# The sparse-attention mixer of a three-block fp32 network: negated scores in PSUM, maxima by pair, and a respaced step list

## What is computed

```python
q, kc, vc, ks, vs, kw, vw, gt, cf = split(h @ w_in)        # 8 q heads, 2 kv groups, head_dim 64
gates = sigmoid(gt).reshape(b, t, 8, 3)
q, ks, kw = rope(rms_norm(q)), rope(rms_norm(ks)), rope(rms_norm(kw))
# compressed branch: 15 blocks of 32 tokens (stride 16), flattened to 2048
kc = rms_norm(gelu(blocks(rope(kc)) @ cmp_w1[0]) @ cmp_w2[0])
vc = gelu(blocks(vc) @ cmp_w1[1]) @ cmp_w2[1]
o_cmp = masked_softmax(q @ kc.T / 8, block_end <= pos) @ vc
# with 256 tokens all 4 selection blocks are chosen and the window covers all: both plain causal attention
o_slc = softmax(q @ ks.T / 8 + causal) @ vs
o_win = softmax(q @ kw.T / 8 + causal) @ vw
o = gates[0] * o_cmp + gates[1] * o_slc + gates[2] * o_win
# convolution branch
z = a * sigmoid(b)                                          # a, b = split(cf), 512 channels each
z = silu(layer_norm(causal_dwconv(z, conf_dw /* 31 taps */) + conf_dw_b))
x = x + concat([o, z]) @ w_out
```

## Time and profile before

| | |
|---|---|
| median of three timed runs | 1105.21 us (1097.91, 1105.21, 1107.57) |
| profiled execution, device time | 1110.08 us |
| its span | 1108.3 us |
| mean granted TensorE clock | 0.950 |
| TensorE busy | 1030.8 us, 93% |
| VectorE, ScalarE, GpSimd busy | 613.7, 492.9, 194.7 us |
| chain that ended last | TensorE 83%, VectorE 6%, ScalarE 5%, GpSimd 3% |

### The profile page before, as it was taken

The page is one execution under the profiler, slowest core; times in us unless marked ns, Lnnn a source line. Parts: engine busy times, 40 slices in busy tenths (PEclk is TensorE's granted clock), DMA queues, the critical chain, the costliest instruction groups (busy, mean ns, idle before and its releaser), DMA issues.

```text
span 1108.3 us, 16443 instructions
## 1 busy us (share of the span) xinstructions
PE 1030.8 (93%) x6750; PEld 916.6 (83%) x6750; DVE 613.7 (55%) x830; ACT 492.9 (44%) x688; POOL 194.7 (18%) x185
## 2 busy tenths in 40 slices
PE   5998999999898888879999998999999999699998
PEld 5987999999788677669999997777777778699996
DVE  4764554454587694345454455455655555755664
ACT  5335444344444443444344344455554545345452
POOL 0006910000122021100000000333442503400000
PEclk9998999999898795699999999999999999899999
DMA  8653565656554320034655665454435543544260
GB/s 277 197 174 115 190 190 184 194 185 192 162 183 150 114 75 2 1 113 142 195 186 175 194 212 172 147 171 134 143 123 171 159 146 107 160 154 136 93 227 39
DMA packets 120273, 168.61 MB, mean 152 GB/s; under 512 B 6356, under 2 KB 89364, under 8 KB 120212
## 3 DMA queue, kind: packets, MB, share of 16 engines
q1 hardware_dynamic: 119776, 167.58, 47.0%
q10 hardware_dynamic: 436, 0.19, 0.1%
HBM read 165.29 MB, written 2.46 MB: 151 GB/s over the span
## 4 chain that ended last, share of the span: by engine, by line
PE 83%; DVE 6%; ACT 5%; POOL 3%; issue 2%; DMA 1%; SPq 0%; DVEq 0%; ACTq 0%; POOLq 0%
PE ps L397 25%; PE ps L399 24%; PE ps L398 24%; PE ps L635 3%; PE ps L609 2%; PE ps L623 2%; ACT scratch_sb L673 1%; DVE scratch_sb L1097 1%; DVE wlo_sb L386 1%; POOL sinv_sb L462 1%; PE ps L785 1%; ACT whi_sb L380 1%; POOL scratch_sb L1986 1%; DMA scratch_sb<-conf_dw 1%; POOL b_inv_sb L1980 1%
## 5 line engine op out<-in xcount | busy, mean ns | idle before, releaser
L386 DVE TENSOR_TENSOR wlo_sb<-raw_sb,whi_sb 128x2048 fp32r<-128x2048 f32 x150 | 345.2, 2301 | 220.7 <-ACT whi_sb L380 220.6
L380 ACT ACTIVATE whi_sb<-raw_sb 128x2048 fp32r<-128x2048 f32 x150 | 287.0, 1914 | 201.2 <-PE ps L399 198.1
L397 PE MATMUL ps<-hhi_sb,whi_sb 128*128 128x256 f32 x1088 | 310.0, 285 | 11.0 <-DVE qkl_sb L1867 7.2
L398 PE MATMUL ps<-hlo_sb,whi_sb 128*128 128x256 f32 x1088 | 308.1, 283 | 0.0
L399 PE MATMUL ps<-hhi_sb,wlo_sb 128*128 128x256 f32 x1088 | 307.5, 283 | 0.0
L397 PEld LDWEIGHTS ps<-hhi_sb,whi_sb 128*128 128x128 f32 x1088 | 209.2, 192 | 14.8 <-DVE wlo_sb L386 7.4
L398 PEld LDWEIGHTS ps<-hlo_sb,whi_sb 128*128 128x128 f32 x1088 | 209.2, 192 | 0.8
L399 PEld LDWEIGHTS ps<-hhi_sb,wlo_sb 128*128 128x128 f32 x1088 | 209.0, 192 | 0.0
L397 PE MATMUL ps<-whi_sb,hhi_sb 128*128 128x512 f32 (+1 forms) x336 | 135.0, 402 | 1.5 <-DVE hlo_sb L479 1.4
L398 PE MATMUL ps<-wlo_sb,hhi_sb 128*128 128x512 f32 (+1 forms) x336 | 131.1, 390 | 0.0
L399 PE MATMUL ps<-whi_sb,hlo_sb 128*128 128x512 f32 (+1 forms) x336 | 131.1, 390 | 0.0
(11 more groups left out here) (270 smaller groups left out, 1237.1 us busy)
## 6 DMA issues: line engine op xcount, KB each, us to landing
raw_sb<-w_in SPq DMA_DIRECT2D x45, 1024.0 KB, 5.3
raw_sb<-ffn_gate SPq DMA_DIRECT2D x22, 1024.0 KB, 5.3
raw_sb<-ffn_up SPq DMA_DIRECT2D x22, 1024.0 KB, 5.2
raw_sb<-ffn_down SPq DMA_DIRECT2D x22, 1024.0 KB, 4.9
raw_sb<-w_in_odd SPq DMA_DIRECT2D x9, 1024.0 KB, 5.2
raw_sb<-w_in_even SPq DMA_DIRECT2D x8, 1024.0 KB, 7.1
raw_sb<-w_branch SPq DMA_DIRECT2D x6, 1024.0 KB, 5.1
scratch_sb<-bias_rows_dram SPq DMA_DIRECT2D x40, 128.0 KB, 2.7
```

The lines of the kernel that those rows point to most:

```text
L380: nc.scalar.activation(whi[:, n0 % SPLIT, :], raw[:, n0 % RAW, :], ACT.Copy).then_inc(hi_ready, 1)
L386: nc.vector.tensor_tensor(wlo[:, n0 % SPLIT, :], raw[:, n0 % RAW, :], whi[:, n0 % SPLIT, :].bitcast(F32), ALU.subtract).then_inc(lo_ready, 1)
L397: nc.tensor.matmul(dst, l_hi, r_hi, start=first, stop=False)
L398: nc.tensor.matmul(dst, l_hi, r_lo, start=False, stop=False)
```

## The change

Nothing outside the odd mixer changes. In it:

1. **Scores.** q's scale is negative, so that PSUM holds negated scores. The mask is added by TensorE: one product of the identity with the negated 128 x 128 mask, both as float32r copies that ScalarE writes into `hhi[:, 2]` (`ident_r`, `mask_r`). Only the last 128 columns need it. VectorE takes the minimum of both heads in one reduction from PSUM, ScalarE's exponentials read PSUM. Pairs alternate between banks 0, 1 and 2, 3, and the transposes go into the pair's own first bank. So scores of pair p wait for the copy of pair p-2, no longer for VectorE's operation on p-1.
2. **Order.** The compressing tiles are whole at steps -2, 0, 6 and 8 (before: -2, -1, 2, 3); the wait for q and k moves behind the first. The tiles are split at other steps (`SPLIT_STEP`). The fourth group's convolution goes one step in two, from 1 to 27. VectorE does two taps a step. `rope_k` and its sums go ahead of a split, both token copies and flat blocks one tile earlier.
3. **Tail.** Layer norm, second branch sum and output rows leave the step list (now -2 to 32) and stand behind it. Output rows begin with the attention half. The last value products are weighted out of PSUM by VectorE, GpSimd keeps one of that sum's products. ScalarE's table loads for the root and for Silu are triggered ahead of their waits by operations on one column.

```diff
+        ident_r, mask_r = hhi[:, 2, 0:P], hhi[:, 2, P:T]
...
+        def pair_s1(pe, p):
+            if p >= 2:
+                pe.wait_ge(pT_copied, p - 1)
+            two, b = jobs1[2 * p:2 * p + 2], 2 * (p % 2)
+            w = len(two[0][5]) * P
+            for e, (qh, ql, kh, kl, bias, v, g, col) in enumerate(two):
+                nc.tensor.matmul(ps[:, b + e, 0:w], qh, kh, start=True, stop=False)
+                nc.tensor.matmul(ps[:, b + e, w - P:w], ident_r, mask_r, start=False, stop=False)
+                nc.tensor.matmul(ps[:, b + e, 0:w], qh, kl, start=False, stop=False)
+                nc.tensor.matmul(ps[:, b + e, 0:w], ql, kh, start=False, stop=True).then_inc(s_ready, 1)
+
+        def pair_max1(dve, p):
+            g, col, b = jobs1[2 * p][6], jobs1[2 * p][7], 2 * (p % 2)
+            w = len(jobs1[2 * p][5]) * P
+            dve.wait_ge(s_ready, 2 * p + 2)
+            nc.vector.tensor_reduce(nmax[:, g, col:col + 5:4], ps[:, b:b + 2, 0:w], AX.X,
+                                    ALU.min).then_inc(s_shifted, 2)
+
+        def pair_exp1(act, p):
+            act.wait_ge(s_shifted, 2 * p + 2)
+            if p >= 2:
+                act.wait_ge(pT_ready, p - 1)
+            for e in range(2):
+                qh, ql, kh, kl, bias, v, g, col = jobs1[2 * p + e]
+                w = len(v) * P
+                nc.scalar.activation(pr[:, 2 * (p % 2) + e, 0:w], ps[:, 2 * (p % 2) + e, 0:w], ACT.Exp, scale=-1.0,
+                                     bias=nmax[:, g, col:col + 1],
+                                     accum_out=psum_[:, g, col:col + 1]).then_inc(p_ready, 1)
...
-        CMP_STEP, HT_STEP, GELU_STEP, W2_STEP = (-2, -1, 2, 3), (1, 7), (2, 8), (6, 12)
-        KCT_STEP, SC_STEP, PCT_STEP, OC_STEP = 14, (16, 24), (19, 27), (21, 29)
-        FIN_STEP, SUM_STEP, OT_STEP = (21, 33), (22, 34), (23, 35)
-
-        LN_MEAN, LN_DEV, LN_SQ, LN_VAR, LN_ROOT, LN_NORM, LN_SILU, LN_LO = 24, 24, 25, 25, 26, 27, 28, 29
-        GROUP_STEP = (8, 16, 24, 32)
-        STEPS1, ROWS_STEP, SPLIT_STEP = range(-2, 36), 33, 15
-        CONV3_STEP = range(1, 15)
+        PAIRS1 = len(jobs1) // 2
+        CMP_PART = {-2: (0, 0, KC), 0: (1, 0, KC), 6: (2, 0, KC), 8: (3, 0, KC)}
+        SPLIT_STEP = {-2: CMP + 2, 2: CMP + 3, 7: OUT1, 13: OUT1 + 1}
+        HID_STEP, HT_STEP, GELU_STEP, TANH_STEP, W2_STEP = (3, 13), (4, 14), (5, 15), (7, 17), (9, 19)
+        KCT_STEP, SC_STEP, PCT_STEP, OC_STEP = 16, (17, 25), (21, 29), (23, 31)
+        FIN_STEP, OC_SUM_STEP, SUM_STEP, OT_STEP = (20, 31), (24, 32), 26, 31
+        GROUP_STEP, CONV3_REST = (8, 16, 24), 30
+        STEPS1, CONV3_STEP = range(-2, 33), range(1, 28, 2)
...
             for m in STEPS1:
+                if m in CMP_PART:
+                    cmp_part(*CMP_PART[m])
+                if m == -2:
+                    pe.wait_ge(qk_lo, 3)
+                    pe.wait_ge(th_ready, 2)
+                    pe.wait_ge(z_ready, 4)
+                    pe.wait_ge(z3_hi, 2)
+                if m % 2 == 0:
+                    p = m // 2
+                    if p + 1 < PAIRS1:
+                        pair_s1(pe, p + 1)
+                    if 0 <= p < PAIRS1:
+                        pair_t(pe, jobs1, 0, p, 0, 2)
+                    if p >= 1:
+                        pair_pv(pe, jobs1, 0, p - 1)
...
+            pe.wait_ge(conf_step, 3 * CONF_K)
+            pe.wait_ge(conv3_step, CONF_K - PE_TAPS + 1)
+            channel_mean(zc, T)
+            branches_T(1)
+            pe.wait_ge(ln_sq, 1)
+            channel_mean(dsq, 0)
             pe.wait_ge(oT_lo, 2)
-            out_rows(2, 0, False, False)
-            out_rows(3, 2, False, True)
+            out_rows(0, 0, True, False)
+            out_rows(1, 2, False, False)
+            pe.wait_ge(z_lo, 1)
+            out_rows(2, 4, False, False)
+            pe.wait_ge(z_lo, 2)
+            out_rows(3, 6, False, True)
...
             for t in range(9):
+                if t == 7:
+                    dve.wait_ge(u_copied, 4)
+                    for i in range(NT):
+                        rope_k(i)
+                        sums_u(1, i)
                 split_lo(dve, N_MIX1 + t + 2)
...
-                conf_taps((0, 3, 6, 6, 0, 4, 4, 0, 2)[t])
-            flat_low(0)
+                    flat_low(0)
+                    flat_low(1)
+                conf_taps((0, 3, 6, 5, 0, 1, 4, 2, 3)[t])
...
-                conf_taps(3, 3 * CONF_K)
+                conf_taps(2, 3 * CONF_K)
+            dve.wait_ge(fin_v, 2)
+            dve.wait_ge(fin_p, 4)
+            nc.vector.tensor_tensor(oacc[:, 1, :], oacc[:, 1, :], ot[:, 0, :], ALU.add).then_inc(fin_v, 1)
+            dve.wait_ge(pv_done, PAIRS1)
+            weighted(ot[:, 1, :], O_BANK, 1, 2, o_copied)
+            dve.wait_ge(o_copied, 4)
+            dve.wait_ge(fin_v, 3)
+            nc.vector.tensor_tensor(oacc[:, 1, :], oacc[:, 1, :], ot[:, 1, :], ALU.add).then_inc(oacc_ready, 1)
```

More of the change, by code:

```diff
@@ L114, in tile_list @@
         mix1 += [c[:, 0:8, :], c[:, 8:16, :]]
-    mix1 += [rows(a["w_out_odd"][0], r) for r in (2, 3, 0, 1)]
+    mix1 += [rows(a["w_out_odd"][0], r) for r in range(4)]
     return mix0, mix1
@@ L799, in conv3, with cmp_part @@
                     mm.then_inc(conv3_done, 1)
[L801 to L808, removed]
+            def cmp_part(row, k0, k1):
+                kv, half = row // 2, row % 2
+                n = CMP + row
+                if k0 == 0:
                     pe.wait_ge(lo_ready, n + 1)
@@ L811, in mix1_pe, with branches_T @@
                     pe.wait_ge(tok_ready, 8)
-                    if r == 2:
+                    if row == 2:
                         pe.wait_ge(hidt_copied, 1)
[L814 to L819, removed]
-                    mm.then_inc(tile_used, 1)
-                if m % 2 == 0 and m <= len(jobs1):
-                    pe_step(pe, jobs1, 0, m // 2)
+                hi, lo = w_parts(n, KC)
+                for k in range(k0, k1):
+                    fh = flat_part(yhi, kv)[:, 8 * half + k, :]
+                    fl = flat_part(ylo, kv)[:, 8 * half + k, :]
+                    mm = product(ps[0:2 * N_CMP, 6, 0:T], fh, fl, hi[:, k, :], lo[:, k, :],
+                                 half == 0 and k == 0, half == 1 and k == KC - 1)
+                if k1 == KC:
+                    mm.then_inc(tile_used, 1)
+            def branches_T(i):
+                pe.wait_ge(oacc_ready, i + 1)
+                if i:
+                    pe.wait_ge(oT_lo, 1)
+                for c in range(4):
+                    mm = nc.tensor.transpose(ps[:, 7, c * P:(c + 1) * P], oacc[:, i, c * P:(c + 1) * P], ident[:, :])
+                mm.then_inc(oT_done, 1)
+            for m in STEPS1:
+                if m in CMP_PART:
[13 more added lines that the diff above has]
+                        pair_pv(pe, jobs1, 0, p - 1)
                 if m in CONV3_STEP:
@@ L1293, in mix1_dve @@
[L1293 to L1294 removed]
+                if m in OC_SUM_STEP:
+                    compressed(OC_SUM_STEP.index(m))
+                if m == SUM_STEP:
+                    dve.wait_ge(fin_v, 1)
+                    dve.wait_ge(fin_p, 3)
+                    nc.vector.tensor_tensor(oacc[:, 0, :], oacc[:, 0, :], ot[:, 0, :], ALU.add).then_inc(oacc_ready, 1)
+                if m == OT_STEP + 1:
+                    branches_lo(0)
+                if m == CONV3_REST:
```

242 lines of the change are left out of this document (110 added, 132 removed).

## The result

Nine runs of the changed kernel have a median of 1114.5 us (1109.3 to 1120.9); nine of the kernel before, on the same chip, 1105.2 (1097.9 to 1111.3). The ratio is **1.0084, 95% interval 1.0052 to 1.0115**: slower, by less than one per cent. The forecast was 1107, its range 1088 to 1117.

A forecast was written before the change was run, and what follows sets the result against it. TensorE (93% busy) was taken as the bound, losing to waits on VectorE, then arithmetic at 1.2 GHz. The stretch summed to 492.7 against 490.92, +1.8 us, set on the 1105.2 median: 1107 us, range 1088 to 1117.

The forecast's parts named there:

- Start: Start of the stretch: first compressing tile no longer waits for q and k; TensorE starts at 356.96, 3.98 us earlier.
- The score group: From pair 9, half clock: six products 0.95 us plus two mask products 0.30; 1.25 a group, seven groups, 8.8.
- D: Rival: 128-row mask products break up the score group, near +10 us, 1117; decided by a group over 1.9; chance 0.18.
- The round: One pair in the loop, scores to copy and hand-over: 2.35 us at 128 columns; at 256, about 3.3 at full clock.
- The rounds with a split: Steps 2, 7 and 13, where ScalarE's and VectorE's splits stand between: 5.8, 6.5 and 6.9 us.
- The gap before pair 9: TensorE has nothing from 398.0 to 402.1, 4.1 us; half clock is taken for the rest.
- The gap of 3.6 us forecast at 370 us: Early rounds: TensorE out of work from 370.0 to 373.6, until the copy of pair 1, ending at half clock.
- From pair 9 on: Pair 9's scores at 402.1 to the last value product: TensorE's list at half clock, sum 56.7 us, to 458.8.
- rival B: The clock comes back in the loop or doesn't fall: put at 1090 us; chance 0.27, of it 0.20 faster.
- The convolution's 7.7 us: From pair 9: six of fourteen pairs of taps, spread to step 27, 1.28 us a step at half clock, 7.7.
- Rival C: Late taps ride free if TensorE isn't the bound after pair 9: the 7.7 us go, 1099; chance 0.09.
- The tail: Two means of 3.73 us, subtraction and square between, to 468.6; output rows 22.9 plus 1.2, to 492.7.

The follow-up runs named there:

- e5: The changed kernel (mask products in the middle) with the convolution's pairs of taps back at steps 1 to 14; ratio 1.0117 to the kernel before.
- e6: The changed kernel with mask products last and the convolution's pairs of taps back at steps 1 to 14; ratio 0.9956 to the kernel before.
- e9: The changed kernel with mask products last and the second output tile's split put behind the loop; 1085.8 us, ratio 0.9822 to the kernel before.
- e10: e9 with the splits of the fourth compressing tile and first output tile moved from steps 2 and 7 to 5 and 9; ratio 0.9889 to before.

## Why the prediction was right, and where it was wrong

The forecast was a change of under one per cent at 1107 us, and 1114.5 lies within its range, near the upper end. That is partly luck: the price of the score group failed by far, and the clock's return in the loop, which the forecast had left to a rival, hid it. The prediction's own signs say so. A score group of 2 us was to make it wrong by far, and it took 2.76; pair 9's scores came later than before and not earlier; the clock was at full speed for 13.7 us where it was to stay at half. By the prediction's own steps, for the profiled execution, each from its own head transposes (355.24 us before, 356.62 after):

```
                                        predicted   measured    off
head transposes to pair 9's scores        46.9        53.0     +6.1
pair 9's scores to the first mean         56.7        54.9     -1.8
first mean to the next transposes         35.4        33.2     -2.2
stretch                                  139.0       141.1     +2.1
```

- **Start: right.** The first compressing tile begins 1.23 us behind the head transposes begin, 5.70 before; 4.5 us won, 4.0 predicted, and the 1.0 us wait for q and k behind the tile was 1.18.
- **The score group: wrong, and the step that failed.** "I take 0.30" for two mask products, "fully exposed they would be 0.58 each". Measured, they add 1.8 us to a group at half clock, 1.1 at full: 0.9 each, beyond the upper bound. The bound asked what a mask product takes; it had to ask what the products around it lose. The argument against D, that the groups "already alternate 64-row halves without a break", was the evidence for it: the forecast counts six 256-column products of the convolution as 1.28 us at half clock, 0.21 each, and has six score products of as many columns in 0.95, which can only be if some run side by side. D's own test, a group over 1.9 us, was met.
- **The round: wrong for the same reason.** 3.27 us from score group to score group at 128 columns (396.21 to 399.48, the clock full), not 2.35: 0.8 of the 0.9 us between them is the group, the rest hand-overs; VectorE had been idle for 1.26 us when its maximum began, so its taps weren't in the way. With the masks last the round is 2.62 (386.39 to 389.01). So pair 9 came 6.1 us later than predicted, counted from the head transposes, and 3.3 later than before. The rounds with a split came as worked out (5.6, 6.4 and 6.85 us from copy to copy for 5.8, 6.5 and 6.9). The gap before pair 9 was 2.64 us, not 4.1, and ended at half clock as taken. The gap of 3.6 us forecast at 370 us wasn't there: TensorE waited 0.61 and 0.46 us, and the clock stood at half from 371.6 to 385.3 us all the same.
- **From pair 9 on: the sum near by luck, both parts off.** Seven score groups took 16.1 us, not 8.8, or 7.3 more. The rest of the list took 38.9, not 47.9, or 9.0 less, as the clock came back from 426.2 to 439.9 us: rival B in part, and by its own argument, the convolution between the scores. In e5 and e6, with the convolution early, the clock didn't come back there.
- **The convolution's 7.7 us: no cost.** Its work was on TensorE, in six steps of 1.56 us or 0.89 where 1.28 was counted; taken out again, nothing is won (e5) or 3.9 us lost (e6). Rival C had this right for the wrong reason: TensorE was the bound (20.50 of 20.50 us busy from 439.90), and what the taps cost, the clock gave back.
- **The tail: right**, 2.2 us better than the sum: the means took 3.0 and 2.9 us, not 3.7 each, for the granted clock over them was 0.60 and 0.56 and not 0.50, and the output rows ran unbroken in 23.1 (473.03 to 496.17), 24.1 predicted.
- **What the stretch doesn't explain.** The ratio says 9.3 us, the two traces 4.9: 3.9 in the stretch (137.2 to 141.1), 1.4 ahead of it, -0.4 behind. The other 4.4 us are the baseline: before's profiled execution lies 4.9 us above its median and after's 0.5. Before's ran at a mean clock of 0.950, near the low end of the 81 runs of that kernel beside the experiments, whose times go with the clock (0.964 in one of 1096.5 us, 0.956 to 0.958 in the middle, 0.949 in three of 1111). After's, 0.949, is the median of its own. The forecast worked its difference out in an execution that lay 4.9 us above the median and then set it on the median. Of the 7.5 us by which 1107 was low, 4.4 are the baseline, 2.1 the stretch and 1.0 the rest of the kernel, which had been put at nothing.

The rest of the change is worth having, which D hid: with only the masks' place mended it is 0.8% faster than before.

## What to carry to other kernels

Two heads in two 64-row halves of TensorE cost the time of one, until any 128-row product stands between them: keep such a run of products together and put what uses all rows at its end. Before pricing an added instruction, divide a group's time by its count; if that is below the spacing at which such products start in one stream (0.16 against 0.21 us here), some run side by side, and the price of a newcomer includes what it ends of that. A gap of 3 to 4 us on TensorE was followed by 8 us of mostly half clock where dense products came next (e9) and by 24 us where they didn't (e10), 3.3 us of the stretch and 7 of the medians, so look at what follows before moving a gap; and compare the profiled execution's clock with that of the timed runs before adding a difference to a median.

## What the runs showed that was not expected

- The overlap is complete: six products of 256 columns in 0.94 us at half clock, three in 0.93.
- Across the two halves, products don't start in the order of the code. It has L690 of the first head ahead of L687 of the second, and the trace starts them at 410.88 and 410.50. That is why six products that are issued one head after the other can run in twos.
- The granted clock came back inside a loop of scores, transposes and value products when six convolution products stood in each second step (0.99 from 426 to 440 us), and didn't without them (0.50 to 0.54 over 43 us).
- It also fell with almost no idle time: in the changed kernel it read 0.51 in the early rounds (371.6 to 385.3 us), where TensorE's waits were 0.6 and 0.5 us, between the long score groups.
